# Attention scores kept with the opposite sign: a minimum in place of a maximum and its negation

## The reference

```python
s = jnp.where(mask, s, -jnp.inf)
m = jnp.maximum(jnp.max(s, axis=-1, keepdims=True), sink)
e = jnp.exp(s - m)
pr = e / (jnp.sum(e, axis=-1, keepdims=True) + jnp.exp(sink - m))
o = pr @ v          # then the output projection w_o and the residual
```

## Time and profile before

| | us |
|---|---|
| median of 3 runs | 4957.7 |
| lowest and highest of them | 4950.1 and 4960.78 |
| the profiled execution's own time | 4956.04 |
| its span, from the first to the last instruction | 4954.3 |
| attention, from its first DVE instruction to the next phase (2500.7 to 3253.0) | 752.3 |

### The profile page before, as it was taken

How to read it: one execution, slowest core, us unless ns; L and a number is a source line. 1 busy time by engine, 2 the same in 40 slices (tenths; PEclk the granted TensorE clock), 3 DMA queues, 4 the chain that set the end, 5 groups by cost and what they waited for, 6 DMA issues and landing times. The chain is left out here.

```text
span 4954.3 us, 93219 instructions
## 1 busy us (share of the span) xinstructions
PE 4502.6 (91%) x29795; PEld 2854.9 (58%) x30217; DVE 2891.0 (58%) x5879; ACT 2043.1 (41%) x2994; POOL 1631.1 (33%) x1161
## 2 busy tenths in 40 slices
PE   7985999999996799999959988986999999997999
PEld 6953676766664344444435555544766776664444
DVE  6775454544444566665579988973444444443666
ACT  6844443343332333333245555534443434331343
POOL 1104444353441111111034444403444534331332
PEclk9988999999998899999979999998999999998999
DMA  8968899988885888888689888958888988885664
GB/s 244 323 230 285 278 299 279 291 290 268 271 287 160 222 223 219 223 224 225 155 188 213 200 207 192 212 185 289 281 289 277 290 289 279 283 270 157 229 234 168
DMA packets 1262631, 1204.88 MB, mean 243 GB/s; under 512 B 925856, under 2 KB 961696, under 8 KB 1262496
## 3 DMA queue, kind: packets, MB, share of 16 engines
q1 hardware_dynamic: 1216416, 1069.05, 73.1%
q0 software_dynamic: 46080, 134.27, 8.2%
HBM read 742.77 MB, written 274.73 MB: 205 GB/s over the span
## 5 line engine op out<-in xcount | busy, mean ns | idle before, releaser
L837 POOL TENSOR_TENSOR ex_w_lo<-ex_raw,ex_w_hi 128x2048 bf16<-128x2048 f32 x192 | 780.7, 4090 | 1101.3 <-ACT ex_w_hi L896 1101.2
L896 ACT ACTIVATE ex_w_hi<-ex_raw 128x2048 bf16<-128x2048 f32 x384 | 707.1, 1900 | 385.9 <-PE ex_ps_y L112 189.6
L1008 PE MATMUL ex_ps_gate<-ex_xT,ex_w_hi 128*128 128x0 bf16 x2048 | 565.9, 277 | 140.4 <-DMA ex_xT<-ex_xrow 105.6
L1009 PE MATMUL ex_ps_gate<-ex_xT,ex_w_hi 128*128 128x0 bf16 x2048 | 565.5, 276 | 0.0
L1010 PE MATMUL ex_ps_gate<-ex_xT,ex_w_lo 128*128 128x0 bf16 x2048 | 565.4, 276 | 0.0
L1008 PE MATMUL ex_ps_up<-ex_xT,ex_w_hi 128*128 128x0 bf16 x2048 | 558.2, 273 | 0.0
L1009 PE MATMUL ex_ps_up<-ex_xT,ex_w_hi 128*128 128x0 bf16 x2048 | 558.2, 273 | 0.0
L1010 PE MATMUL ex_ps_up<-ex_xT,ex_w_lo 128*128 128x0 bf16 x2048 | 558.2, 273 | 0.0
L988 DVE COPY ex_y<-ex_ps_y 128x512 f32 x324 | 224.2, 692 | 566.9 <-PE ex_ps_y L112 564.6
L972 DVE TENSOR_TENSOR ex_aT<-ex_silu,ex_ps_up 128x384 bf16<-128x384 f32 x256 | 141.8, 554 | 679.9 <-PE ex_ps_up L1010 500.4
L111 PE MATMUL ex_ps_y<-ex_w_lo,ex_aT 128*128 128x512 bf16 x1296 | 492.2, 380 | 8.5
(11 more groups left out here) (348 smaller groups left out, 9188.5 us busy)
## 6 DMA issues: line engine op xcount, KB each, us to landing
ex_raw<-in_w_exp_gate SPq DMA_DIRECT2D x128, 1024.0 KB
ex_raw<-in_w_exp_up SPq DMA_DIRECT2D x128, 1024.0 KB, 12.5
ex_raw<-in_w_exp_down SPq DMA_DIRECT2D x128, 1024.0 KB, 6.0
y_rows<-ex_y SPq DMA_DIRECT2D x162, 512.0 KB
up_rows<-rt_up_out SPq DMA_DIRECT2D x64, 512.0 KB, 2.6
cb_hin<-h_mid SPq DMA_DIRECT2D x64, 512.0 KB, 4.0
cb_up_in<-up_rows SPq DMA_DIRECT2D x64, 512.0 KB, 4.7
mix_x<-in_x SPq DMA_DIRECT2D x32, 512.0 KB, 5.5
```

Source lines behind the costliest of these rows:

```text
L837: eng.tensor_tensor(w_lo[u][:, w], raw[:, c, :], w_hi[u][:, w], ALU.subtract).then_inc(lo_done, 1)
L896: act.activation(w_hi[u][:, c * WCHUNK:(c + 1) * WCHUNK], raw[:, c, :], ACT.Copy).then_inc(hi_done, 1)
L1008: pe.matmul(out, hi, x_hi, start=j == 0, stop=False)
L1009: pe.matmul(out, hi, x_lo, start=False, stop=False)
```

## The change

The scores are written to SBUF with the sign turned (the reduction's `scale` is now -1), VectorE reduces their minimum instead of their maximum, against a sink that is negated once at the start, and the exponential reads the turned scores with a scale of -1 and that minimum as its bias. The instruction that negated the maxima is gone, and with it the tile `mx`, the semaphore `mx_done` and VectorE's wait for its own reduction; PE's `scores` waits on `nmx_done` in its place. The last columns of the score tiles are filled from the negated sink.

```diff
@@ exps
-                    e = act.activation(ex[c % ER][:, k, :], score[c][:, k, :], ACT.Exp, bias=nmx[:, n:n + 1],
+                    e = act.activation(ex[c % ER][:, k, :], score[c][:, k, :], ACT.Exp, scale=-1.0, bias=nmx[:, n:n + 1],
                                        accum_out=esum[:, n:n + 1])
@@ sinks
                 dve.wait_ge(sink_loaded, 16)
+                dve.tensor_scalar(sink[:], sink[:], -1.0, None, ALU.mult).then_inc(sink_turned, 1)
+                dve.wait_ge(sink_turned, 1)
                 for c in range(NP):
@@ top
                     last = dve.tensor_tensor_reduce(out=score[c][:, k, 0:W], in0=ps_s[:, c % 2, k, :], in1=mask[:],
-                                                    scale=1.0, scalar=sink[:, head(c, k):head(c, k) + 1], op0=ALU.add, op1=ALU.max,
-                                                    accum_out=mx[:, n:n + 1])
-                last.then_inc(mx_done, 1)
-                dve.wait_ge(mx_done, pairs(t, c))
-                dve.tensor_scalar(nmx[:, 2 * c:2 * c + 2], mx[:, 2 * c:2 * c + 2], -1.0, None, ALU.mult).then_inc(nmx_done, 1)
+                                                    scale=-1.0, scalar=sink[:, head(c, k):head(c, k) + 1], op0=ALU.add, op1=ALU.min,
+                                                    accum_out=nmx[:, n:n + 1])
+                last.then_inc(nmx_done, 1)
@@ scores
-                wait(pe, mx_done, pairs(t, c - 2))
+                wait(pe, nmx_done, pairs(t, c - 2))
```

More of the change, by code:

```diff
@@ L1801, in attention_phase @@
         prT = [m.sb(f"prT{jj}", [P, 8, HALF, P], BF16) for jj in (0, 1)]
-        mx, nmx, esum, rden = (m.sb(n, [P, NQ]) for n in ("mx", "nmx", "esum", "rden"))
+        nmx, esum, rden = (m.sb(n, [P, NQ]) for n in ("nmx", "esum", "rden"))
         oT = m.sb("oT", [P, 2, KD, P], BF16)
@@ L1818, in attention_phase @@
         k_ld, v_ld = ([m.sem(f"{n}{r}") for r in range(KR)] for n in ("k_ld", "v_ld"))
-        s_mm, top_open, mx_done, nmx_done, e_done, rden_done, ph_done, pl_done, turn_open = m.sems(
-            "s_mm top_open mx_done nmx_done e_done rden_done ph_done pl_done turn_open")
+        s_mm, sink_turned, top_open, nmx_done, e_done, rden_done, ph_done, pl_done, turn_open = m.sems(
+            "s_mm sink_turned top_open nmx_done e_done rden_done ph_done pl_done turn_open")
         pT_turned = [m.sem(f"pT_turned{i}") for i in range(ER)]
```

## The result

The changed kernel takes 4926.9 us, the median of four runs (4922.3 to 4933.3), against 4959.2 for the kernel before in the same session: a ratio of 0.9939 with a 95% interval of 0.9927 to 0.9952, or 32 us less. The forecast was 4927. The profiled execution of the changed kernel is the slowest of its four (4933.3, span 4931.5), so its span is compared stage by stage only.

A forecast was written before the change was run, and what follows sets the result against it. A loop through VectorE, ScalarE and PE was taken to bind each 21.2 us attention tile. 22.4 us without the clock plus 8.2 for fewer clock falls gave 30.6, so 4927 us, range 4916 to 4945.

The forecast's parts named there:

- 8.2 for the clock: Five fewer falls of TensorE's granted clock behind its longer wait (4 in 28 tiles instead of 9), 1.65 us each.
- (a): Where VectorE is free to go on after the accumulator read, removing the negation saves 0.20 us.
- (b): The signal to ScalarE comes from the read's end instead of the negation's, 0.20 us earlier.
- (c): Where the negation runs into a GpSimd instruction on the shared port, the port rule alone returns all of its 0.40 us.
- (d): At pairs 0, 1, 2 and 4 `rests` needs GpSimd's result, so removed time becomes waiting; counted as nothing.
- Loop 2: Binding tile loop through VectorE's `top(4)`, ScalarE's `out_hi` and PE's second-half projection: 21.2 us to become 20.35.
- P0: Start of PE's first-half `project`; its 1.20 us wait for ScalarE's `out_hi` was to shrink to some 0.80.
- P1: Start of PE's second-half `project`; its 0.48 us wait for ScalarE's `out_hi` was to come near to nothing.
- falls end: Rival: all nine clock falls vanish, gain 37.3 us, time 4920; chance 0.24.
- if the stall keeps its length: Condition for 0.85 us gained in each of five loop-turn tiles, where VectorE stands 3.6 us on average.
- All of it comes out: Rival: the removed negations' whole time is gained, 256 x 0.238 = 61 us, time 4897; chance 0.02.
- no shorter path: Rival: `rests` waits for GpSimd everywhere, so nothing is gained, time 4957; chance 0.06.

The follow-up runs named there:

- slot_back: Changed kernel with a 128x2 negation put back behind each pair's two reductions, waiting for them but writing a tile nobody reads: 4939.5 us.
- op_alone: Changed kernel with a 128x2 negation of the sink's ready columns behind each pair's reductions, without a wait, its output read by nobody: 4928.5 us.
- flat_after: Changed kernel with attention's loop written out on VectorE alone, the other engines keeping their loop: 4897.5 us.
- padded kernels: Changed kernel with tiny unread copies on VectorE ahead of the loop: 4919.9 us with 33 copies, 4927.5 us with 80 copies.

## Why the prediction was right

**The size.** 30.6 us were summed, 32 came. By kinds of tile, from the step ends of both traces: the 23 tiles without the turn fell from 497.0 us to 470.0, 27.1 less, where the terms 15 x 0.85, 8 x 0.40 and 8.2 for the clock give 24.2. The five with the turn fell by 1.1 us in all, where 5 x 0.85 = 4.25 was put. The start gave 4.3 where 0.85 + 1.3 = 2.15 was put. Two terms too small and one too large, together 2 us. Ordinary tiles came as they were worked out. That the median lies within 0.1 us of the forecast is luck all the same: the clock gave back more than was put, and the turn took 8.7 us that were put at nothing.

**(a), the slot.** 0.20 was right for its size, and slot_back shows that it counts. Its reason was not spelt out: 0.12 of it is VectorE's wait for its own read, 0.07 the negation's own place in the list (slot_back and op_alone).

**(b), the signal.** Shown by slot_back: 0.28 a tile for the signal alone; the working had 0.20 for pair 4 and the earlier `out_hi` beside it.

**(c) and (d), GpSimd.** At the four places of (d) nothing came out: in both traces `rests` starts 0.03 us behind GpSimd, and as long behind the accumulator read as before (medians of 0.37 and 0.38, 0.20 and 0.20, 0.44 and 0.44, 0.44 and 0.44 us behind c = 0, 1, 2 and 4). The new idle time of the view, 31.9 us in 92 pieces, stands behind c = 0, 2 and 4, one in each of the 28 tiles; behind c = 1 it is 0.12 us, too short for that view, except in one tile. At c = 3, 5 and 6, where GpSimd had been done, the 0.19 went to nothing. At c = 7, the place of (c), 0.29 of the 0.40 came back: `out_lo` starts 0.14 behind the read in place of 0.43, and is then released by `out_hi`, which ended 0.03 earlier (2645.40 and 2645.43). op_alone, 0.43 there again, shows that the hold is what cost it.

**The loop that binds.** Loop 2 was put at 20.35, measured are 20.37; P0 was put at 0.80, measured are 0.59 with eight recorded matmuls, 0.80 with seven; at P1 nothing is left, as predicted.

**The clock.** This step was mis-sized: four falls behind P0 were put, on a straight line between the ends; there is none in this trace, nor in three more kernels with the same wait. The rival "falls end" was right about the clock. Its 4920 did not come, above all because of the next term. The five waits at P1 of the tiles with the turn did not stay as they were either: 1.64 became 1.05 to 1.13 (1.26 to 1.34 with seven records), and the clock fell behind none. Two falls are left in this trace, in two of these tiles, beside waits of 1.98 and 2.47 us of PE for `top`.

**The turn.** The condition "if the stall keeps its length" did not hold: 18.1 us became 26.8, 1.7 a turn, and "longer than 4.0" was named as a sign that would make the prediction wrong. It took 8.7 us back. That the stall comes with the branch is shown by flat_after; why this change brought the longest of all is shown by the instruction queue, two transfers in each stall in place of one, and by the padded kernels, where it is one again. In the rows the stall counts from the end of the work before it: in the changed kernel VectorE's last operation started at 2686.80 and the next at 2692.66, 5.86 us; with 33 instructions more ahead of the loop it is 2685.01 and 2689.24, 4.23 us, in the kernel before 2691.59 and 2695.24, 3.65 us.

**The start.** Its gain is twice what was put. The mean clock ahead of the first step end is 0.77 before and 0.78 after, so the clock explains little of it. In the runs the same stretch takes 81.5 us with the slot put back and 81.1 with the arithmetic alone, so most of the 4.3 is the slot; which of the preparation's rounds gave it was not tried.

**The rivals that lost.** The reduction as a minimum is not slower (a mean of 479 ns over 475 of them, against 476 before). "All of it comes out" and "no shorter path" are excluded by (d) and by the tiles of 20.37.

## What to carry to other kernels

A small operation that waits for the result ahead of it on its own engine does not cost its duration (0.17 us): look at the start of the next instruction. Here that was 0.12 for the wait and 0.07 for the operation, and up to 0.43 where GpSimd held it; both went by choosing signs so that the reduction's own result is what the consumer needs. Price an edit by the loop that binds, with the engine that is next at each place; where another engine ends the wait anyway, nothing comes out. And look at what a loop's backward branch costs on the engine that binds: here writing out one engine's loop was worth nearly as much again as the change (29 us).

## What the runs showed of the hardware

At its backward branch VectorE stands 3.2 to 5.7 us each time, and goes on 1.7 to 1.9 us behind the last transfer of 8192 bytes of the instruction queue: one transfer in 35 turns, two in 15. For ScalarE and GpSimd, which turn as often, the view of waits has no such stall; one that is hidden behind a wait for VectorE would not show there. The Trainium skill, page "Runtime: NRT & Kernel Launch", section "Instruction fetch mechanics", says that a taken branch out of the fetched window has to fetch its target by DMA first. That the stall goes away with the branch, and holds such transfers, agrees; that the same loop stalls 0.3 to 1.3 us less a turn (means of five, against three kernels) when its code is moved by 33 or 80 instructions is what the runs add.

A semaphore wait on the engine's own last result moved the next VectorE instruction 0.12 us behind the start of the accumulator read (2643.24 and 2643.36 in slot_back), where without one it starts together with the read (2641.36 and 2641.36).

The granted clock of TensorE fell to 1.2 GHz beside waits of 0.9 to 1.4 us in some tiles and not in others that look alike; with one wait of 0.80 in none of 97.

A missing matmul record turns into 0.21 us of apparent waiting: compare the counts (x7, x8) before comparing two waits.
